# Gated delta net: projection tiles of rounds two to four in three fp32r passes, and the first tokens' score sets ranked by fours

## The reference

```python
z = xn @ w_in                                   # xn: (256, 1024)
qkv = silu(causal_depthwise_conv(qkv, conv_w))  # 4 taps
q, k = l2norm(q) * DK ** -0.5, l2norm(k)        # 8 heads of 128
# per chunk of 64 tokens: unit lower triangular solve, then the state recurrence
sol = triangular_solve(lower, rhs)
o = o * rsqrt(mean(o * o) + EPS) * norm_w * silu(z_gdn)
# PEER: 8 heads x 2 halves of 128 keys
s = einsum('bthsc,hsnc->bthsn', q, sub_keys)
top_s, top_i = top_k(s, 16)                     # 16 score sets a token
cand = top_s[..., 0, :, None] + top_s[..., 1, None, :]
best_s, best_pos = top_k(cand, 16)
gate = softmax(best_s)
```

## Time and profile before

| | |
|---|---|
| median of 3 runs | 3546.79 us (3537.99 to 3549.24) |
| profiled execution, its own time | 3549.54 us |
| its span, first to last instruction | 3547.7 us |
| mean granted TensorE clock | 0.966 of full |
| TensorE busy | 3296.1 us (93%) |
| VectorE busy | 2087.9 us (59%) |
| ScalarE busy | 1563.6 us (44%) |
| moved by DMA | 433.19 MB, 122 GB/s |

### The profile page before, as it was taken

One profiled execution on the slowest core, in us unless ns is written; L12 is line 12 of the kernel. 1 busy time (PEld: TensorE's weight loads), 2 busy tenths in 40 slices (PEclk: granted clock), 3 DMA queues, 4 the chain that ended last, 5 costly groups with the idle time before them and its releaser, 6 DMA issues. The chain is left out here.

```text
span 3547.7 us, 73463 instructions
## 1 busy us (share of the span) xinstructions
PE 3296.1 (93%) x24844; PEld 2866.4 (81%) x24844; DVE 2087.9 (59%) x4609; ACT 1563.6 (44%) x3367; POOL 156.6 (4%) x169
## 2 busy tenths in 40 slices
PE   7999989988999999999889999899889999999997
PEld 6777777767988799999777777777689888999996
DVE  4666556541887655555456665555419865555554
ACT  4444343221177555555445443522212865555554
POOL 0100001100000000000001100010000000000000
PEclk9999979999999999999999999899999999999999
DMA  3222222213313555555332222222233235555553
GB/s 123 92 86 72 99 66 91 94 60 149 107 60 104 191 185 184 187 189 188 133 108 75 97 84 87 66 90 83 78 131 107 71 117 186 184 188 189 185 184 116
DMA packets 122227, 433.19 MB, mean 122 GB/s; under 512 B 15744, under 2 KB 18048, under 8 KB 121344
## 3 DMA queue, kind: packets, MB, share of 16 engines
q1 hardware_dynamic: 122112, 431.74, 35.5%
HBM read 430.64 MB, written 1.05 MB: 122 GB/s over the span
## 5 line engine op out<-in xcount | busy, mean ns | idle before, releaser
L244 PE MATMUL bank<-arena,ring 128*128 128x256 f32 x2624 | 629.8, 394 | 52.5 <-PEq L196 13.2
L244 PEld LDWEIGHTS bank<-arena,ring 128*128 128x128 f32 x2624 | 501.0, 196 | 134.4 <-issue 43.8
L2218 DVE TENSOR_TENSOR u_parts<-u_raw,u_parts 128x512 fp32r<-128x512 f32 x384 | 265.8, 693 | 447.8 <-ACT u_parts L2163 447.8
L2163 ACT ACTIVATE u_parts<-u_raw 128x512 fp32r<-128x512 f32 x384 | 242.2, 631 | 519.3 <-PE bank L2102 519.3
L2100 PE MATMUL bank<-xhigh,u_parts 128*128 128x256 f32 x1536 | 433.8, 282 | 2.1 <-DVE u_parts L2218 2.1
L2102 PE MATMUL bank<-xhigh,u_parts 128*128 128x256 f32 x1536 | 434.7, 283 | 0.0
L2101 PE MATMUL bank<-xlow,u_parts 128*128 128x256 f32 x1536 | 434.6, 283 | 0.0
L2100 PE MATMUL bank<-v_parts,act_high 128*128 128x512 f32 x1024 | 406.2, 397 | 12.0 <-DVE v_parts L2223 11.9
L2101 PE MATMUL bank<-v_parts,act_high 128*128 128x512 f32 x1024 | 403.3, 394 | 0.0
L2102 PE MATMUL bank<-v_parts,act_low 128*128 128x512 f32 x1024 | 400.8, 391 | 0.0
L2223 DVE TENSOR_TENSOR v_parts<-v_raw,v_parts 128x512 fp32r<-128x512 f32 x512 | 330.1, 686 | 26.6 <-ACT v_parts L2170 23.9
(11 more groups left out here) (346 smaller groups left out, 5362.1 us busy)
## 6 DMA issues: line engine op xcount, KB each, us to landing
v_raw<-in_v SPq DMA_DIRECT2D x256, 512.0 KB, 3.4
u_raw<-in_u SPq DMA_DIRECT2D x192, 512.0 KB, 4.5
ring<-in_w_side SPq DMA_DIRECT2D x80, 512.0 KB, 3.4
ring<-in_w_gdn SPq DMA_DIRECT2D x64, 512.0 KB, 3.4
ring<-in_w_rwkv SPq DMA_DIRECT2D x48, 512.0 KB, 6.1
ring<-in_w_gdn_side SPq DMA_DIRECT2D x32, 512.0 KB, 3.4
ring<-in_u SPq DMA_DIRECT2D x32, 512.0 KB, 3.8
u_ring<-in_u SPq DMA_DIRECT2D x32, 512.0 KB, 3.3
```

Of the source, the lines that this page charges most:

```text
L244: mm = te.matmul(ps, ring[:, slot, k * P:(k + 1) * P], x[:, k, :], start=(k == 0), stop=(k == KT - 1))
L2163: a_.activation(f32r(u_hi[:, half(n)]), u_raw[:, r % 2, half(n)], ACT.Copy).then_inc(u_high, 1)
L2218: v.tensor_tensor(f32r(u_lo[:, half(n)]), u_raw[:, r % 2, half(n)], u_hi[:, half(n)], ALU.subtract).then_inc(u_low, 1)
```

## The change

In the gated delta phase the tiles of rounds two to four go through `Split` instead of `project`. ScalarE gets `act_round`, VectorE `vec_rest`, for tile 0 of the next round near the head of each body and for tile `n + 1` ahead of piece `n` in `fill(n)`. The first round's tiles stay fp32 (`first=True`). SyncE now waits by `W.free` (the rest of the tile that was in the slot); for the first round's tiles VectorE raises that semaphore by 16 once it has seen `z7`. The array `O` moves out of the place of `x_parts`, and `sq` shares its place with arrays used later in the round. In the ranking, the first 128 tokens' sets are ranked in four calls of four sets, each after its own group of scores; the second 128 tokens' as before.

```diff
-        VA, SA, EA = steps("gdA_vec", True), steps("gdA_act", True), steps("gdA_pe", True)
+        VA, SA, EA = steps("gdA_vec", True), steps("gdA_act", True), steps("gdA_pe")
+        W = Split("gd")
...
-        sq, rs = r_(4, T), r_(4, T)
+        rs = r_(4, T)
...
+        sq = Region(r_.at_)(4, T)
...
             def _(sp):
                 for s in range(4, 8):
-                    sp.wait_ge(EA.sem, EA.at(f"z{s - 4}", 0))
+                    sp.wait_ge(EA.sem, EA.at(f"z{s - 4}"))
                     tile_a(sp, l, 0, s)
                 with sp.Fori(1, NI) as i:
                     for s in range(4):
-                        sp.wait_ge(EA.sem, EA.before(f"z{s + 4}", i))
+                        W.free(sp, 8 * i + s - 4)
                         tile_a(sp, l, i, s)
                     for n in range(3):
                         sp.wait_ge(EG.sem, EG.before(f"g{n}", i))
                         tile_g(sp, l, i, n)
                     for s in range(4, 8):
-                        sp.wait_ge(EA.sem, EA.at(f"z{s - 4}", i))
+                        W.free(sp, 8 * i + s - 4)
                         tile_a(sp, l, i, s)
                     sp.wait_ge(EG.sem, EG.before("g3", i))
                     tile_g(sp, l, i, 3)
                 for s in range(4):
-                    sp.wait_ge(EA.sem, EA.at(f"z{s + 4}", NI - 1))
+                    W.free(sp, 8 * NI + s - 4)
                     merge_tile(sp, l, s)
...
                     if part == 0:
-                        te.wait_ge(loaded[s % 4], 32 * i + 16 * (s // 4) + 16)
+                        if first:
+                            te.wait_ge(loaded[s % 4], 16 * (s // 4) + 16)
...
-                    mm = project(te, ps_a[s], s % 4, ks=range(2 * part, 2 * part + 2))
-                    if part == 3:
-                        mm.then_inc(EA.sem, EA.one(f"z{s}"))
+                    if first:
+                        mm = project(te, ps_a[s], s % 4, ks=range(2 * part, 2 * part + 2))
+                        if part == 3:
+                            mm.then_inc(EA.sem, EA.one(f"z{s}"))
+                    else:
+                        W.project(te, ps_a[s], 8 * i + s, s % 2, part)
+
+            def act_round(a, i, s):
+                a.wait_ge(loaded[s % 4], 32 * i + 16 * (s // 4) + 16)
+                W.round(a, ring[:, s % 4], 8 * i + s, s % 2)
+
+            def vec_rest(v, i, s):
+                W.rest(v, ring[:, s % 4], 8 * i + s, s % 2)
...
             def act_body(a, i, more):
                 def fill(n):
+                    if more and n < 7:
+                        act_round(a, i + 1, n + 1)
                     if more:
                         act_piece(a, i + 1, n)
...
                 S.begin()
+                if more:
+                    act_round(a, i + 1, 0)
                 a.wait_ge(SA.sem, SA.at("z7", i))
...
             def vec_body(v, i, more):
                 def fill(n):
+                    if more and n < 7:
+                        vec_rest(v, i + 1, n + 1)
                     if more:
                         vec_piece(v, i + 1, n)
...
                 v.tensor_copy(GB, ...)
+                if more:
+                    vec_rest(v, i + 1, 0)
                 v.wait_ge(S.sem, S.at("silu", i))
...
                 lru.vector(v, lambda s: vec_piece(v, 0, s))
                 VA.end()
+                v.wait_ge(EA.sem, EA.at("z7"))
+                v.sem_inc(W.low, 16)
...
-                    v.wait_ge(SQ.sem, SQ.at("s3", i))
-                    best16(NS, scores[:, i], left, top, topi)
+                    for g in range(4) if i == 0 else (3,):
+                        some = slice(4 * g if i == 0 else 0, 4 * g + 4)
+                        v.wait_ge(SQ.sem, SQ.at(f"s{g}", i))
+                        best16(some.stop - some.start, scores[:, i, some], left[:, some], top[:, some], topi[:, some])
```

More of the change, by code:

```diff
@@ L1216, in gdn_phase @@
         va4 = r_(4)
-        assert r_.at_ <= GDN_ROOM
-        r_ = Region(MIXER)
         O = r_(NB, 2, P)
         O4 = O.rearrange("p b h c -> p (b h) c")
+        assert r_.at_ <= GDN_ROOM
         b2, b3, b4, b5, b6, b7 = banks[2:8]
@@ L1291, in vec_side, with act_piece @@
                 v.tensor_tensor(z, z, ps_g[n], ALU.mult).then_inc(VG.sem, VG.one(f"g{n}"))
-            def act_piece(a, i, s):
+            def act_piece(a, i, s, first=False):
                 if s == 0:
@@ L1297, in act_piece @@
                     a.wait_ge(E.sem, E.before("vT", i))
-                a.wait_ge(EA.sem, EA.at(f"z{s}", i))
+                if first:
+                    a.wait_ge(EA.sem, EA.at(f"z{s}"))
+                else:
+                    W.done(a, 8 * i + s)
                 if s < 6:
@@ L1321, in fill @@
                         pe_piece(te, i + 1, n, (range(3), range(3, 4))[y])
-                if more:
-                    EA.begin()
                 EG.begin()
@@ L1412, in pe_body @@
                 EG.end()
-                if more:
-                    EA.end()
             @block.tensor
@@ L1423, in _ @@
                 mm.then_inc(E0.sem, E0.one("ab"))
-                EA.prime(te)
                 E.prime(te)
                 EG.prime(te)
-                EA.begin()
+                te.sem_inc(W.used, W.PRIME + 16)
                 pe_piece(te, 0, 0, first=True)
@@ L1504, in _ @@
                 S.prime(a)
+                a.sem_inc(W.high, 16)
                 SA.begin()
-                lru.scalar(a, lambda s: act_piece(a, 0, s))
+                lru.scalar(a, lambda s: act_piece(a, 0, s, first=True))
                 SA.end()
```

## The result

The changed kernel takes 3587.5 us (median of 4 runs, 3578.4 to 3591.2) against 3548.0 for the kernel before on the same chip (4 runs): a ratio of 1.0114, 95% interval 1.0087 to 1.0140. It is **slower by 39.5 us**; the forecast had the direction, and 22 us. The profiled execution spans 3585.5 us, 37.8 more than before.

The account below looks back on a forecast made before the run. It took each round as a chain through all engines, then a TensorE-bound part. Head +18.7, clock +6.8, shorter pieces -6.6, ranking -7.9 made +11.0 a layer, +22 us: 3569 us, range 3547 to 3583.

Parts of the forecast that it names:

- The wait for tile 0: Second and third round heads: silu waits for tile 0's landing, copies and its table load, +7.1 and +8.1 us.
- first head: First round's head: next tiles wait until VectorE has seen the last fp32 tile, silu +3.5 us.
- the place of the first table load: Round head: the copies' 1.28 us table load was to run while ScalarE waits anyway; only silu's load was charged.
- shorter pieces: Gated-delta projection tiles in three fp32r passes: 2.2 us gained a round, -6.6 us a layer.
- stall: TensorE waits for tile 1's rest on VectorE in fill(0): 2.1 us a round, 1.6 if bounded by the rest.
- level periods: Inversion's levels: a period falls from 5.5 to 5.0 us, with VectorE's and ScalarE's added work hidden.
- The head's clock: TensorE's gap before the sums leaves half clock: 1.6 us first round, 2.6 in two others, +6.8 a layer.
- The ranking: Ranking by fours: TensorE's early tiles limit the gain to 6.9 us, plus 1 of clock, -7.9 a layer.
- Rival 4: Ranking by fours brings the full 12 us: 10 us less, 3559 us; chance 0.06.
- Rival 1: Round heads: waits as computed, but the clock costs nothing and silu keeps its table: +1, 3548 us; chance 0.18.
- Rival 2: Round heads: tile 0 is in the ring before ScalarE wants it: 3528 us, 3518 if wholly hidden; chance 0.12.
- Rival 3: Inversion's levels: VectorE, not TensorE, sets them, each next tile's rest 0.5 us late: +15, 3584 us; chance 0.06.

Follow-up runs that it names:

- silu-first kernel: Changed kernel plus a one-column silu on ScalarE at each preparing round's head, before the wait for tile 0 and its copies: 3565.9 us, ratio 1.0052.
- best kernel: Changed kernel with next-round tiles issued before the g3 wait, tile 0's copies behind silu, its rest behind the squares, products L1586/L1587 behind tiles 3 and 4: 3509.0 us.
- filled-gap: Changed kernel with 14 unused fp32 matmuls on TensorE at the head of each of the six rounds: 3577.8 us, ratio 1.0087.
- round-behind: Changed kernel with next-round tiles issued before the g3 wait, tile 0's copies moved behind silu and its rest behind the squares: 3537.6 us, ratio 0.9941.
- tiles early: Changed kernel with only SyncE's queue reordered, tiles 0 to 3 of the next round issued before the wait for side product g3: 3546.2 us, ratio 0.9987.
- tile 1's rest early: Changed kernel with VectorE's products L1586 and L1587 moved from in front of tile 1's rest to behind tiles 3 and 4: 3567.3 us, ratio 1.0035.
- the reorder alone: Changed kernel with tile 0's copies moved behind silu and its rest behind the squares, SyncE's queue unchanged: 3534.6 us, ratio 0.9944.

## Why the prediction was right in direction and short in size

- **The wait for tile 0: right.** The profile of before had the two facts, a transfer issued only at the round's end and 5 to 6 us of flight, and the change put silu behind them. Silu near 608 in the second round was forecast, on a first head at 533; it was 614.4, on a first head at 535.0 and a round of 79.4 instead of 76.
- **The failed step: the place of the first table load.** I wrote that the load of L262 "goes in the head while ScalarE waits anyway". It stands behind the wait: 1.28 us more at each of six heads, 7.7 us. The earlier trace rows gave its existence and its price but not its place; I took the place from the earlier trace rows, where silu's load precedes silu's last wait. The same trace had the other place as well, in the fourth round: silu's load at 735.15, behind the wait. In the silu-first kernel both loads leave the path, and the time falls by 21.6.
- **The Trainium skill's rule**, "ScalarE: Activation LUTs", section "Table sets", that a copy needs no load of its own, agrees with the copies at 603.44 and 602.71 above, which follow silu's table without a load. It does not hold for the first operation of the body, which had one each time (20 loads of L262). My text weighed rule against row as if one had to win; each holds in its place. Another page, "ScalarE activation tables: per-element evaluation and per-set limits", section "Table sets in the compiler and the runtime", says that the loads are placed block by block, each for the longest run that one set can serve. The first half agrees with the six new loads at the six bodies' heads, and with the RWKV phase, which has 16 rounds, 14 of them inside its loop, and 14 loads of L262. By the second, one load should have served the two copies and silu; the rows at 610.64 and 613.10 show two, and the measurement decides.
- **The second failed step: the term "shorter pieces", -2.2 us a round.** It was made of 4.7 gained, 2.1 stall, 0.4 lost. Gain less loss, forecast 4.3, was 4.5 by the best kernel; the stall was 2.2, and the level periods fell from 5.5 to 4.95 us as forecast. Missing was 1.5 us of half clock *behind* the stall: the round got 0.8 us, not 2.2 (layer 1: -2.3 for three rounds, not -6.6), 8 to 9 us in all. I had computed the stall and the clock gate each, and asked only at the head whether the one sets off the other. In the changed kernel's profile the fall came in all six rounds; in the filled-gap and round-behind kernels the same wait brought it in two and four of six, so this term is a likely cost of the wait, not a sure one.
- **The head's clock: right** (6.2 a layer, 6.8 forecast; filling the gap gave back 9.8 us). The sum is partly luck: I had the rounds the wrong way about, and the first head, with the shortest wait, paid most (2.4 against 2.0 and 1.8, forecast 1.6, 2.6 and 2.6).
- **The first head: +5.4, forecast +3.5.** Its landing took 3.6 us, in the band. Of the difference, 1.3 is the table load of the failed step and 1.1 came from ahead of the edit; a landing in the lower half of the band gives the rest back.
- **The ranking: right.** -15.3 us in the median against -15.8; TensorE's early tiles are next in line, not VectorE. Rival 4 is out.
- **Rival 1** (no clock cost, silu keeps its table) is refuted by the rows at 611 to 621 and 613.10. **Rival 2** (tile already landed) would have been true of another queue order: with tiles early the kernel ran in 3546, not 3528, for the two loads stay, the first heads still pay clock, and so does each round behind tile 1. **Rival 3** (VectorE bound) is refuted by rounds of 64.0 with two more products in the levels.
- By the sum: 22 forecast, +7.7 for the loads, +9 for the second half-clock stretch gives 39; measured 39.5 in the medians. In the ledger of layer 1 the miss of 8.8 us is 3.8 for the loads, 4.3 for the rest of the rounds and 1.1 from ahead of the edit, less small terms that came out below the forecast, so the close sum owes something to terms that cancel. The range ended at 3583 because its bounds allowed more clock at the head, but no load in a place where I had put none and no second fall of the clock.

## What to carry to other kernels

When a copy is put in front of a function on ScalarE at the head of a loop's body, count two table loads behind the copy's wait, as here; put it behind the function, or load the function's table with a one-column call before the wait. Wherever an edit makes TensorE wait a few microseconds, price the wait and then ask what the clock does behind it, at every such place of the round (behind this one it fell in 35 of 42 rounds). An operation that waits for a transfer belongs behind the work that doesn't need it: the order alone was worth 53 us between the medians here, and the change that lost 1.1% won 1.3% once its loads, copies and subtractions stood in the right places.

## What the runs showed of the hardware that I had not expected

- A wait of 2.17 us in the middle of a round was followed by a granted clock of 0.50 from within 641 to 642 until about 645; TensorE had been busy 0.68 of the 3.00 us up to 641. With tile 1's rest early the wait was gone and the clock stayed at 1.00 in the rows at 633 to 639. But the same wait with the same 0.68 us of work ahead of it left the clock at 1.00 in other rounds (557.70 to 564.70 of the filled-gap kernel). The Trainium skill, "TensorE: Matmul & The Clock Gate", section "HAM oscillation", has a transfer's wait in each pass of a loop make each pass begin at the low clock. The three heads behind the landing agree (9.50, 9.08 and 8.91 us from silu to reciprocal, not 7.08); behind tile 1's wait, which is shorter and for VectorE, it was most rounds and not each.
- A table load was put ahead of a plain copy at a body's head, behind the copy's wait for the transfer, 1283 ns each time; none ahead of the same copies in the middle of a body.
- The executions of one kernel differ by their half clock: the reorder alone ran from 3524.7 us at a mean granted clock of 0.972 to 3546.9 at 0.962, on one chip.
- The flight of the first tile of a burst of four, 512 KB, was 3.6 us at the first head of the changed kernel, where nothing was issued shortly before it, and 5.1 to 5.7 us at its four other heads, where a side tile was issued 1 us earlier (4.5 to 5.9 over the kernels before, changed and silu-first). Whether the side tile is the reason was not tried.
